# Forget-gate heads by seven block products, convolution behind the heads, queries in the last head, and weight sums on GpSimd

## The reference

```python
q, z_f, z_b, v, g = (tile h of projections 0, 1, 2, 3, 4)     # per head h, 8 heads of 128
k = (1 - lb) * sigmoid(-z);  log_f = logaddexp(log lb, log1p(-lb) + log_sigmoid(z))
o = chunk scan over tokens, context first, forward (z_f) and backward (z_b)
a_lat = rmsnorm(o_f + o_b) * silu(g)
b_lat = p5 * depthwise_conv3(p6 * p7)                         # projections 5, 6, 7
c_lat = attention(rope(rmsnorm(p8)), keys, values)            # 16 heads, 4 key heads, 768 keys
y = sigmoid(ga) * (a_lat @ Wa) + sigmoid(gb) * (b_lat @ Wb) + sigmoid(gc) * (c_lat @ Wc);  x += gate * (y @ Wout)
```

## Time and profile before

| | us |
|---|---|
| median of 3 runs | 3518.42 (3510.56 to 3518.65) |
| the profiled execution | 3516.85 |
| its span | 3514.9 |
| TensorE busy | 3219.8 (92%) |
| VectorE busy | 1186.6 (34%) |
| ScalarE busy | 746.2 (21%) |
| GpSimd busy | 14.9 (0%) |
| first projection tile of head 0 | 73.11 |
| attention's first score | 1015.09 |

### The profile page before, as it was taken

One profiled execution on the slowest core, in us unless ns is written; L12 is line 12 of the kernel. 1 busy time (PEld: TensorE's weight loads), 2 busy tenths in 40 slices (PEclk: granted clock), 3 DMA queues, 4 the chain that ended last, 5 costly groups with the idle time before them and its releaser, 6 DMA issues.

```text
span 3514.9 us, 33716 instructions
## 1 busy us (share of the span) xinstructions
PE 3219.8 (92%) x13475; PEld 1971.5 (56%) x13475; DVE 1186.6 (34%) x1978; ACT 746.2 (21%) x1412; POOL 14.9 (0%) x31
## 2 busy tenths in 40 slices
PE   5999999996999999996899997888999998889998
PEld 3555655555465444444343433344888855468886
DVE  1343344444246200014001013051555424345543
ACT  3222223333247300011000002242000013310001
POOL 0000000000000000000000000000000000000000
PEclk9999999997999999997999999999999998999999
DMA  5133223332310112022999993201121211012221
GB/s 221 48 144 144 97 106 133 144 138 109 133 57 1 48 73 92 26 100 103 420 405 411 409 413 134 92 16 48 72 96 72 96 74 48 25 72 86 82 96 48
DMA packets 63636, 451.45 MB, mean 128 GB/s; under 512 B 7200, under 2 KB 7216, under 8 KB 10128
## 3 DMA queue, kind: packets, MB, share of 16 engines
q1 hardware_dynamic: 60624, 439.38, 31.1%
q0 software_dynamic: 2080, 7.04, 0.6%
q10 hardware_dynamic: 800, 3.15, 0.2%
HBM read 445.34 MB, written 2.10 MB: 127 GB/s over the span
## 4 chain that ended last, share of the span: by engine, by line
PE 78%; DVE 7%; DMA 6%; ACT 4%; issue 2%; DVEq 2%; PEld 1%; PEldq 0%; SPq 0%; ACTq 0%
PE PS L195 71%; DMA arena<-stream 3%; DMA xT<-stream 1%; PE PS L1063 1%; PE PS L1171 1%; DMA ring<-stream 1%; PE PS L1154 1%; DMA arena<-ctxt 1%; DVE arena L1125 1%; DVE stat L1180 1%; PEld PS L195 1%; PE PS L1646 1%; DVEq L773 1%; ACT hT L286 1%; PE PS L1626 1%
## 5 line engine op out<-in xcount | busy, mean ns | idle before, releaser
L195 PE MATMUL PS<-arena 128*128 128x256 f32 (+3 forms) x3936 | 803.0, 403 | 69.7 <-DVE arena L803 21.6
L195 PEld LDWEIGHTS PS<-arena 128*128 128x128 f32 (+1 forms) x3936 | 583.8, 186 | 294.1 <-issue 178.1
L195 PE MATMUL PS<-hT,ring 128*128 128x512 f32 (+1 forms) x1632 | 620.3, 539 | 33.6 <-ACT hT L286 18.9
L195 PE MATMUL PS<-arena,ring 128*128 128x256 f32 (+1 forms) x1800 | 561.3, 469 | 4.5 <-ACT arena L1097 2.4
L195 PEld LDWEIGHTS PS<-hT,ring 128*128 128x128 f32 x1632 | 317.3, 196 | 319.8 <-issue 299.0
L195 PEld LDWEIGHTS PS<-arena,ring 128*128 128x128 f32 x1800 | 343.1, 191 | 208.0 <-issue 178.3
L195 PE MATMUL PS<-ring,arena 128*64 128x512 f32 (+3 forms) x1216 | 236.4, 590 | 23.6 <-ACT arena L1457 9.0
L195 PE MATMUL PS<-hT,xT 128*128 128x512 f32 x576 | 250.7, 592 | 0.0
L195 PEld LDWEIGHTS PS<-hT,xT 128*128 128x128 f32 x576 | 108.5, 190 | 130.9 <-issue 130.9
L195 PEld LDWEIGHTS PS<-ring,arena 128*64 128x64 f32 (+2 forms) x1216 | 82.5, 131 | 163.0 <-issue 154.9
L1491 DVE TENSOR_TENSOR arena<-arena,PS 128x512 f32<-128x512 f32 x16 | 11.0, 688 | 410.9 <-PE PS L195 410.9
(11 more groups left out here) (266 smaller groups left out, 2771.3 us busy)
## 6 DMA issues: line engine op xcount, KB each, us to landing
ring<-stream SPq DMA_DIRECT2D x277, 1024.0 KB, 7.6
arena<-stream SPq DMA_DIRECT2D x96, 1024.0 KB, 9.4
xT<-stream SPq DMA_DIRECT2D x44, 1024.0 KB, 7.5
arena<-x ACTq DMA_DIRECT2D x1, 2048.0 KB, 19.7
arena<-arena POOLq DMA_DIRECT2D x16, 128.0 KB, 2.6
arena<-x POOLq DMA_DIRECT2D x2, 1024.0 KB, 6.3
out<-arena SPq DMA_DIRECT2D x4, 512.0 KB, 2.6
arena<-ctxt ACTq DMA_DIRECT2D x1, 1024.0 KB, 26.5
```

Source lines behind the costliest of these rows:

```text
L195: ins = nc.tensor.matmul(out_, lhsT, rhs, start=start, stop=stop_, **kw)
```

## The change

- Each head's query, gate and two forget tiles are one block of seven products (part_pe), into banks 0, 1, 4 and 5. TensorE runs products 1 to 4 ahead of the levels, 5 to 7 after level 2; the values come as half units of their own. The activations' sums T_x are made once, in xT (turned_sums).
- The four weight sums of such a block are formed by GpSimd for the eight heads and the two query blocks (sums_pool, last_sum_pool), with three buffers for four sums. VectorE forms them for the six convolution blocks (sums_dve, last_sum_dve, the same operations).
- Convolution tiles (24, six blocks) and the convolution itself move behind the keys and values; queries (two blocks) move into the last head; the last head's modulation chunks move behind it.
- Loops over heads are written out. The next head's prep_act and decays move to the end of the head before. hW is three deep, the 1 x 1 copy L813 goes, and there are five adds out of PSUM per head (mid_dve, ends_dve).
- The ring has four slots and T_x's place up to the merge, then four. Each pair of slots has a semaphore of its own. SyncE waits for x before the first weights; TensorE waits for x, and for ctx only ahead of its own transposes.
- GpSimd's constants for the heads are loaded at once. Swapped halves are double-buffered, tile j+2 after the scores of tile j.

Of each function the added lines and those kept are shown; what they replace stands in the functions printed above.

```diff
+def _early():
+    order = [("c", 0, 0), ("c", 1, 1), ("c", 2, 2), ("c", 3, 1), ("F", 0, 0), ("v", 0, None),
+             ("A", 0, 1), ("F", 1, 0), ("v", 1, None)]
+    for h in range(HG - 2):
+        order += [("A", 4 * h + 1, 1), ("F", h + 2, 0), ("A", 4 * h + 2, 1), ("A", 4 * h + 3, 1),
+                  ("v", h + 2, None), ("A", 4 * h + 4, 1)]
+    h = HG - 2
+    order += [("A", 4 * h + 1, 1), ("Q", 0, 0), ("A", 4 * h + 2, 1), ("A", 4 * h + 3, 1), ("Q", 1, 1)]
+    h = HG - 1
+    order += [("A", 4 * h, 0), ("K", 0, 1), ("A", 4 * h + 1, 0), ("A", 4 * h + 2, 0), ("A", 4 * h + 3, 0)]
+    order += [("B", i, i % 2) for i in range(6)]
+    return order
...
+        def part_pe(pe, n, i):
+            u = quad_unit(n)
+            A, B = weight_blocks(u), halves(hT)
+            if i == 1:
+                unit_wait(pe, u)
+                if n:
+                    pe.wait_ge(p_c, n)
+                w, x, bank = A[0, 0], B[0, 0], 0
+            elif i == 2:
+                pe.wait_ge(p_s, 4 * n + 1)
+                pe.wait_ge(p_t, 1)
+                if n:
+                    pe.wait_ge(p_d, 4 * (n - 1) + 3)
+                w, x, bank = part_sum(n, 0), T_x[:, 0, :, :], 1
+            elif i == 3:
+                pe.wait_ge(p_s, 4 * n + 2)
+                pe.wait_ge(p_t, 2)
+                if n:
+                    pe.wait_ge(p_d, 4 * (n - 1) + 4)
+                w, x, bank = part_sum(n, 1), T_x[:, 2, :, :], 2
+            elif i == 4:
+                pe.wait_ge(p_s, 4 * n + 3)
+                pe.wait_ge(p_t, 3)
+                w, x, bank = part_sum(n, 2), T_x[:, 1, :, :], 3
+            elif i == 5:
+                unit_wait(pe, u + 1)
+                pe.wait_ge(p_x, 2 * n + 1)
+                w, x, bank = A[0, 1], B[1, 0], 0
+            elif i == 6:
+                pe.wait_ge(p_s, 4 * n + 4)
+                pe.wait_ge(p_x, 2 * n + 2)
+                w, x, bank = part_sum(n, 3), B[1, 1], 1
             else:
+                pe.wait_ge(p_t, 4)
+                pe.wait_ge(p_d, 4 * n + 1)
+                w, x, bank = A[1, 1], T_x[:, 3, :, :], 2
+            for t in range(2):
+                for k in range(KH):
+                    last = t == 1 and k == KH - 1
+                    mm(part_bank(bank)[:, t, :], w[:, k, t * P:(t + 1) * P], x[:, k, :],
+                       i <= 4 and t == 0 and k == 0, last, p_p if last else None, skip_group_check=True)
...
+        def sums_pool(pool, n):
+            u = quad_unit(n)
+            A = weight_blocks(u)
+            pool.drain()
+            unit_wait(pool, u)
+            unit_wait(pool, u + 1)
+            if n:
+                pool.wait_ge(p_p, 7 * (n - 1) + 3)
+            nc.gpsimd.tensor_tensor(part_sum(n, 0), A[1, 0], A[1, 1], ALU.add).then_inc(p_s, 1)
+            if n:
+                pool.wait_ge(p_p, 7 * (n - 1) + 4)
+            nc.gpsimd.tensor_tensor(part_sum(n, 1), A[0, 0], A[1, 0], ALU.subtract).then_inc(p_s, 1)
+            if n:
+                pool.wait_ge(p_p, 7 * (n - 1) + 6)
+            pool.drain()
+            nc.gpsimd.tensor_tensor(part_sum(n, 2), part_sum(n, 0), A[0, 0], ALU.subtract).then_inc(p_s, 1)
+        def last_sum_pool(pool, n):
+            pool.wait_ge(p_p, 7 * n + 2)
+            pool.drain()
+            nc.gpsimd.tensor_tensor(part_sum(n, 3), weight_blocks(quad_unit(n))[0, 1], part_sum(n, 2),
+                                    ALU.subtract).then_inc(p_s, 1)
...
+        def mid_dve(v, n, i):
+            if i == 0:
+                v.wait_ge(p_x, 2 * n + 2)
+                v.wait_ge(p_p, 7 * n + 3)
+                nc.vector.tensor_tensor(Up[:, 0, :, :], Xp[:, 1, :, :], part_bank(2), ALU.add).then_inc(p_d, 1)
...
+        def ends_dve(v, n):
+            low, high = quad_out(n)
+            v.drain()
+            nc.vector.tensor_tensor(high[:, :, HN:T], Up[:, 1, :, :], Up[:, 0, :, :], ALU.add)
+            v.wait_ge(p_p, 7 * n + 6)
+            nc.vector.tensor_tensor(low[:, :, HN:T], Up[:, 1, :, :], part_bank(1), ALU.add).then_inc(p_d, 1)
+            v.wait_ge(p_p, 7 * n + 7)
+            nc.vector.tensor_tensor(high[:, :, 0:HN], Up[:, 1, :, :], part_bank(2), ALU.add).then_inc(p_d, 1)
...
+        def head_pe(pe, h):
+            n = h + 1
+            pe.wait_ge(c_e, 3 * n)
+            part_pe(pe, n, 1)
+            part_pe(pe, n, 2)
+            if h:
+                pe.wait_ge(a_e2, 2 * h)
+            part_pe(pe, n, 3)
+            part_pe(pe, n, 4)
+            for lv in range(3):
+                level_pe(pe, h, lv)
             turn_keys(pe, h, 0)
+            for i in (5, 6, 7):
+                part_pe(pe, n, i)
+            if n < HG:
+                ada_products(pe, h, 0)
+            else:
+                quad_done(n)
+            for lv in range(3, 6):
+                level_pe(pe, h, lv)
             turn_keys(pe, h, 1)
+            if n < HG:
+                context_pe(pe, n)
+            else:
+                for i in (1, 2, 3):
+                    part_pe(pe, n + 1, i)
+            level_pe(pe, h, 6)
+            level_pe(pe, h, 7)
+            states_pe(pe, h, 0)
+            if n < HG:
+                ada_products(pe, h, 1)
+                values_pe(pe, n, 0)
+            else:
+                part_pe(pe, n + 1, 4)
+                part_pe(pe, n + 1, 5)
+            states_pe(pe, h, 1)
+            if n < HG:
+                ada_products(pe, h, 2)
+                values_pe(pe, n, 1)
+            else:
+                part_pe(pe, n + 1, 6)
+                part_pe(pe, n + 1, 7)
+                quad_done(n + 1)
+            out_pe(pe, h)
+            if n < HG:
+                ada_products(pe, h, 3)
+                flush(pe)
+            square_sum(pe, h)
+            if n < HG:
+                ada_sums(pe, h)
...
+        def head_dve(v, h):
+            n = h + 1
             v.wait_ge(h_x2, h + 1)
             factors_dve(v, 0)
             factors_dve(v, 1)
...
             nc.vector.tensor_tensor(hQ[:, 1, :].rearrange("p (m t) -> p m t", t=P), ends,
                                     hX[:, DECAY_B, 0:T].rearrange("p (m t) -> p m t", t=P), ALU.subtract)\
                 .then_inc(h_x, 1)
             factors_dve(v, 2)
+            queries_dve(v, h, 0)
+            queries_dve(v, h, 1)
+            mid_dve(v, n, 0)
+            queries_dve(v, h, 2)
+            mid_dve(v, n, 1)
+            for lv in range(3):
+                merge_level(v, h, lv)
+                factors_dve(v, lv + 3)
+            for lv in range(3, 6):
+                queries_dve(v, h, lv)
+            v.wait_ge(h_e, h + 1)
+            q = QG[h % 2][:, 0, :]
+            nc.vector.tensor_tensor(hQ[:, 0, :], hQ[:, 0, :], q, ALU.mult)
+            nc.vector.tensor_tensor(hQ[:, 1, :], hQ[:, 1, :], q, ALU.mult).then_inc(h_qm, 1)
+            if n == HG:
+                ends_dve(v, n)
+            merge_level(v, h, 3)
             factors_dve(v, 6)
+            merge_level(v, h, 4)
+            merge_level(v, h, 5)
+            queries_dve(v, h, 6)
             v.wait_ge(h_k, h + 1)
+            nc.vector.tensor_tensor(hW[:, 1, 0, :], hW[:, 1, 0, :], hW[:, 1, 1, :], ALU.add).then_inc(h_wl, 1)
+            if n < HG:
+                ends_dve(v, n)
+            else:
+                mid_dve(v, n + 1, 0)
+            merge_level(v, h, 6)
+            merge_level(v, h, 7)
+            states_dve(v, h, 0)
+            g = QG[h % 2][:, 1, :]
             v.wait_ge(h_sl, h + 1)
+            nc.vector.scalar_tensor_tensor(hsq, g, 0.0, hsq, ALU.min, ALU.subtract).then_inc(h_sm, 1)
+            if n == HG:
+                mid_dve(v, n + 1, 1)
             v.wait_ge(h_sg, h + 1)
+            nc.vector.tensor_tensor(g, g, hsq, ALU.mult).then_inc(h_gm, 1)
+            if n < HG:
+                decays_dve(v, n, 0)
+                states_dve(v, h, 1)
+                decays_dve(v, n, 1)
             else:
+                states_dve(v, h, 1)
+                ends_dve(v, n + 1)
+            out_dve(v, h)
...
+        def qkv_pe(pe):
+            for j in range(6):
+                if j < 4:
+                    ada_products(pe, HG - 1, j)
+                    flush(pe)
+                kv_pe(pe, j)
+                if j == 3:
+                    ada_sums(pe, HG - 1)
+                item_pe(pe, j)
+            flush(pe)
+            s = 6
+            for c in range(6):
+                n = HG + 2 + c
+                if c == 0:
+                    pe.wait_ge(a_e2, 2 * HG)
+                for i in range(1, 8):
+                    part_pe(pe, n, i)
+                    if i in (2, 4, 6):
+                        item_pe(pe, s)
+                        s += 1
+                quad_done(n)
+            flush(pe)
...
+            s = 6
+            for c in range(6):
+                n = HG + 2 + c
+                last_sum_dve(v, n)
+                mid_dve(v, n, 0)
+                item_dve(v, s)
+                mid_dve(v, n, 1)
+                item_dve(v, s + 1)
+                if c < 5:
```

(42 more changed lines are left out.)

831 lines of the change are left out of this document (441 added, 390 removed).

## The result

| | us |
|---|---|
| kernel before, median of 4 runs | 3517.60 (3510.56 to 3518.65) |
| kernel after, median of 4 runs | 3377.64 (3371.88 to 3385.78) |
| ratio after to before | 0.9608, 95% interval 0.9584 to 0.9632 |
| profiled execution of after | 3371.88, its span 3370.1 |
| forecast | 3391, range 3372 to 3455 |

The change takes 140 us away, 13 more than forecast. The first lines are the page's totals, which answer to the earlier trace rows.

The account below looks back on a forecast made before the run. TensorE was taken to bound the heads, VectorE having slack. 58 + 44 + 497 + 66.5 + 214.5 + 9.5 = 889.5 us to attention against 1015.1, so -125.6; residual -1.5 and clock +1.5 leave 3391 us, range 3372 to 3455.

Parts of the forecast that it names:

- the rival with 0.22: In the heads, VectorE's chain sets the pace: a head costs 79 us, total 3455; chance 0.22.
- The sign named for being wrong: VectorE's 512-wide operations well beyond 0.69 us beside GpSimd with TensorE waiting for states or level queries, or sums over 5 us.
- Start, 58 us: Kernel start: first block at 58 us instead of 73, as TensorE no longer waits for ctx.
- First part, 44: First block, context and values ahead of the heads: 42 us, plus 2 us for its first sums.
- Heads, 71: Seven heads, 71 us each: TensorE's work 67.7, other waits 2.5 (levels, DMA, tail), GpSimd's interference 1.
- Last head, 66.5: Last head: the query blocks cover its chain; only the square sum waits, 1.2 us; 66.5 us in all.
- Behind the heads, 214.5: Modulation chunks, key and value tiles, small products, convolution blocks: 212 us busy, about 2 us of weight waits.
- The hole at attention's start, 9.5 and 1.5 of clock: Before attention's first maximum, convolutions 6 and 7 leave TensorE idle 9.5 us, with 1.5 us for a lower clock behind.
- The output projection, -1.5: Residual behind the merge: four slots let its first weights come earlier, gaining 1.5 us.
- GpSimd's sums: 2.3 us: One 128x1024 weight sum on GpSimd takes 2.3 us, between bounds of 1.22 and 2.3; heads break even at 6.9.
- The place of the sums: In the heads: GpSimd or VectorE gives the forecast time, or 8 us less where nothing interferes.
- the likeliest case: Whole kernel: 3391 us, by itself 3372 to 3410; chance 0.65.

Follow-up runs that it names:

- a_late: Changed kernel, GpSimd's sums of blocks 2 to 8 starting only after the second chain of states: 3365.44 us, ratio 0.9590.
- b_start: Kernel before with only the changed load order at the start (weights wait for x, x turned without waiting for ctx): 3502.40 us, ratio 0.9973.
- a_vsums: Changed kernel with the weight sums of the eight heads and two query blocks on VectorE instead of GpSimd: 3365.32 us, ratio 0.9588.
- c_spread: Changed kernel, head and query sums on VectorE, last two convolutions' ten operations one after every fourth attention unit (4 to 40): 3360.30 us, ratio 0.9564.
- b_unroll: Kernel before with only its loops over pairs of heads written out: 3496.75 us, ratio 0.9957.
- a_eight: Changed kernel with eight products and no weight sums in the blocks of heads and queries: 3396.89 us, ratio 0.9669.
- a_lastbare: Changed kernel with the two query blocks made behind the last head instead of inside it: 3403.12 us, ratio 0.9684.
- a_double: Changed kernel with GpSimd forming the first three sums of each of ten blocks twice: 3415.37 us, ratio 0.9716.

## Why the prediction was right, and by how much it was off

The mechanism and the places were right, and the total came within 0.4% partly by luck: in the set-off at the end of this section the first part and the stage behind the heads cost 8.6 us more than forecast, the heads and the output projection 22.5 less.

**What bounds the kernel: right.** TensorE, in the heads 97% busy, VectorE with room to spare; no chain of VectorE took over (the rival with 0.22), GpSimd stayed far from setting the pace (sums 2.35 to 3.80 us, in a_late up to 4.90, break-even 6.9). The sign named for being wrong came half true: TensorE does wait for states in every head, but no longer than the 2 us that had been allowed for.

**Start, 58 us: right** (58.88). The transposes of x begin at 14.2; b_start shows the same 14.3 us alone. The tenth is luck: the changed kernel's other trace has 63.50.

**Work and idle time.** From the first projection product to the first score the terms take 942 us down to 822 (44 + 497 + 66.5 + 214.5): 55 as work, 65 as idle time. Measured were 942 to 812: 80 (866 to 786 us busy) and 50. The mean granted clock of this stretch was 0.95 before and is 0.99 now, so part of the 80 should be clock, not work; the sum had 848 busy us where the trace of before has 866.

**First part, 44: 47.0.** Three waits for ScalarE's copies (L697, 2.0 us together) and a granted clock of 0.95 were not in the walk.

**Heads, 71: 68.3.** This is where most of the miss lies, in two terms. The 2.5 us of other idle time (levels, DMA, tail) did not come: a head's waits hold the 2.1 us of states and nothing else. And TensorE's work, 67.7, is at most 66.4, the pitch of a_vsums' heads, whose only wait is 0.5 us. It was summed from timeline rows of a head of before; those heads ran at a clock of 0.96 to 0.98 and the new ones at 1.00, and the rows' modelled ends overlap. Which of the two makes the 1.3 us the runs don't tell. The cost of GpSimd was taken at 1, between 0 and 2, and is 2.1 by the wait (1.8 by the pitch), the upper bound, by the mechanism and at the place named: forward decays stretched, states 1 pushed, output products late. Head 0 alone took 70.3, with two waits for levels of 1.30 and 1.22 us.

**Last head, 66.5: 65.4.** The one wait named, the square sum, is there with 1.17.

**Behind the heads, 214.5: 220.1.** Three waits of 0.80, 1.17 and 0.98 us, four of "issue", and TensorE busy 216 where 212 were summed.

**The hole at attention's start, 9.5 and 1.5 of clock: 8.6 together** (171.5 us of attention against 162.9): TensorE is idle 6.2 us more in it, the wait of 7.67 among that, and busy 2.4 more at the lower clock. c_spread shows that all of it was avoidable.

**The output projection, -1.5: -6.9.** From GpSimd's first constants behind the merge to the next ones lay 635.1 us before (1511.39 to 2146.53) and lie 628.2 after; every version with four slots has 628 to 630, those with the old ring 635 to 638. The step had 1.5 of the 2.1 us of wait and left out the 2.8 us of clock that fell behind it. The last 2 us of the 6.9 the rows of this place don't show; where they lie stays open.

**GpSimd's sums: 2.3 us** was right where VectorE leaves it alone (2.35), and 2.4 to 3.2 in the mean: 115 us for the 40 sums instead of 92, and 131.5 instead of about 105 for the engine. The Trainium skill's figure (GPSIMD Engine Reference, 3.1) led to an estimate of 2.25; the trace's shortest sum is within 0.1 of it.

**The place of the sums.** It was called harmless or worth 8 us, inside the likeliest case. Moved to VectorE, or later on GpSimd, it is worth 16 us by the medians and 11 or 14 by the traces up to attention: 1.8 us in each head's pitch, and in a_vsums 4 more ahead of head 0's gate, with 5 lost again in the last head. The bound was in the text; the value chosen within it was not argued from a row.

The forecast of 3391 lies 13 us, 0.4%, above the median and 19 above the profiled execution, for which the terms can be set off: start +0.9, first part +3.0, seven heads -17.1 (479.9 for 497), last head -1.1, behind the heads +5.6, attention's start -2.4, output projection -5.4, all else -2.6.

The change as a whole was not taken apart. b_unroll and b_start account for 16 and 10 us of the 140, and a_eight and a_lastbare for 15 and 21; what the moved convolution tiles and the moved decays are worth by themselves no run shows.

## What to carry to other kernels

Work given to an idle GpSimd is not free for VectorE: look which of VectorE's two-input operations it will fall beside, and whether anyone waits for them; a wait that moves the sums behind that chain was worth as much as taking them off GpSimd. When sums move to another engine, look at every place where they land: in a_vsums they landed in front of a merge of the last head. Price a wait that goes together with the lower clock behind it. And small operations that must go into a stage bound by a chain belong where another engine's long work lies over that chain, not spread evenly.

## What the runs showed that I had not expected

Both engines lose, and not by fair turns: in a_late a sum of 2.35 us took 4.57, for it waited out not one operation of VectorE but four that followed each other without a gap (timelines of GpSimd and VectorE):

```profile
451.10 4.57 POOL L639 TENSOR_TENSOR arena<-ring,arena 128x1024 f32<-128x1024 f32 x1 [7.71 <-PE PS L223]
```

```profile
450.97 0.68 DVE L1002 TENSOR_TENSOR arena<-arena 128x512 f32<-128x512 f32 x1
451.57 0.68 DVE L1004 TENSOR_TENSOR arena<-arena 128x512 f32<-128x512 f32 x1
452.17 1.28 DVE L1011 TENSOR_TENSOR arena<-arena 128x512 f32<-128x512 f32 x2
454.49 0.69 DVE L647 TENSOR_TENSOR arena<-arena,PS 128x512 f32<-128x512 f32 x1 [1.04 <-PE PS L223]
455.10 1.13 DVE L1011 TENSOR_TENSOR arena<-arena 128x512 f32<-128x512 f32 x1
```

The four end at 453.45, and the sum ends 2.2 us behind that, at 455.67. In these 2.2 us L647, which reads one input from PSUM, runs in its usual 0.69 us, while the next L1011, with both inputs in SBUF, takes 1.13 instead of 0.68. a_double shows the same in seven heads: the operations of the states (L1040, one input in PSUM) lie inside a running sum and take 0.35 us each, as they do alone. So in these traces a sum and an operation that reads PSUM cost each other nothing. A copy of SBUF values is not free, though: even one of 128 x 6 values on VectorE, 0.17 us elsewhere, waited out a sum (VectorE's timeline of a_late):

```profile
507.96 2.10 DVE L982 COPY arena<-arena 128x6 f32<-128x6 f32 x1
```

A lost stretch of TensorE can cost more than itself: behind the 2.10 us at the output projection, which came right after 2.23 us of idle time, 16 records took 9.84 us instead of 7.03, and behind a_double's 4.1 us the head lost another 1.5. And a gain that a trace shows to a tenth of a microsecond (5.3 us in c_spread) can drown in the spread of five runs.
